# Odd layer: the band mask and the row extreme of the scores move into one VectorE instruction

## What is computed

```
s = q @ k^T * 64**-0.5                 # a block of 128 queries, up to 384 keys
s = where(|i - j| <= 128, s, -inf)     # the band
m = max(max(s, axis=-1), sink)
p = exp(s - m)
p = p / (sum(p) + exp(sink - m))
o = p @ v                              # then a SiLU gate and the output projection
```

## Time and profile before

| | |
|---|---|
| median of three runs | 1152.68 us |
| span of the profiled execution | 1149.1 us |
| rest of the median, around the span | 3.6 us |
| odd layer's scores, first to last | 735.2 to 1122.5 us in the span |
| PE busy | 1123.6 us, 98% |
| DVE busy | 975.0 us, 85% |
| ACT busy | 677.8 us, 59% |
| granted TensorE clock, mean | 0.996 |

### The profile page before, as it was taken

One profiled execution on the slowest core, in us unless ns is written; L12 is line 12 of the kernel. 1 busy time (PEld: TensorE's weight loads), 2 busy tenths in 40 slices (PEclk: granted clock), 3 DMA queues, 4 the chain that ended last, 5 costly groups with the idle time before them and its releaser, 6 DMA issues. The chain is left out here.

```text
span 1149.1 us, 18542 instructions
## 1 busy us (share of the span) xinstructions
PE 1123.6 (98%) x5752; PEld 912.9 (79%) x5752; DVE 975.0 (85%) x1925; ACT 677.8 (59%) x1326; POOL 0.2 (0%) x4
## 2 busy tenths in 40 slices
PE   7999999999999999999999999999999999999996
PEld 6778778778778778778878867887888888888876
DVE  6889889889889889889889898888888888888886
ACT  6475564564554654654654665366666566666664
POOL 0000000000000000000000000000000000000000
PEclk9999999999999999999999999999999999999999
DMA  7614323323224224224125121545232324323111
GB/s 224 165 37 126 113 74 87 97 73 95 88 73 102 80 73 117 65 73 124 59 73 138 47 74 31 122 129 142 61 91 55 91 68 120 98 63 91 55 38 74
DMA packets 131531, 103.62 MB, mean 90 GB/s; under 512 B 5408, under 2 KB 116384, under 8 KB 131488
## 3 DMA queue, kind: packets, MB, share of 16 engines
q1 hardware_dynamic: 131344, 102.81, 32.5%
q10 hardware_dynamic: 144, 0.26, 0.1%
HBM read 77.88 MB, written 2.10 MB: 70 GB/s over the span
## 5 line engine op out<-in xcount | busy, mean ns | idle before, releaser
L74 PE MATMUL bank_proj<-hH,w_hi 128*128 128x512 f32 x856 | 343.0, 401 | 1.2 <-issue 0.8
L76 PE MATMUL bank_proj<-hH,w_lo 128*128 128x512 f32 x856 | 334.8, 391 | 0.0
L75 PE MATMUL bank_proj<-hL,w_hi 128*128 128x512 f32 x856 | 334.5, 391 | 0.0
L76 PEld LDWEIGHTS bank_proj<-hH,w_lo 128*128 128x128 f32 x856 | 161.0, 188 | 35.3
L74 PEld LDWEIGHTS bank_proj<-hH,w_hi 128*128 128x128 f32 x856 | 161.6, 189 | 32.7 <-issue 1.2
L75 PEld LDWEIGHTS bank_proj<-hL,w_hi 128*128 128x128 f32 x856 | 161.6, 189 | 30.6 <-issue 0.2
L2012 ACT ACTIVATE probs<-bank_odd_score,small 128x256 f32<-128x256 f32 (+1 forms) x128 | 66.3, 525 | 73.0 <-DVE small L2263 73.0
L1253 DVE TENSOR_TENSOR w_lo<-w_raw,w_hi 128x1024 fp32r<-128x1024 f32 x74 | 89.6, 1218 | 0.8 <-ACT w_hi L741 0.7
L2019 ACT ACTIVATE probsT<-bank_odd_turn 128x256 fp32r<-128x256 f32 (+1 forms) x128 | 48.8, 434 | 62.8 <-PE bank_odd_turn L1733 62.7
L741 ACT ACTIVATE w_hi<-w_raw 128x1024 fp32r<-128x1024 f32 x74 | 77.9, 1053 | 0.2
L806 ACT ACTIVATE probs<-bank_score,small 128x512 f32<-128x512 f32 x64 | 43.4, 684 | 55.1 <-DVE small L1091 49.3
(11 more groups left out here) (452 smaller groups left out, 2218.8 us busy)
## 6 DMA issues: line engine op xcount, KB each, us to landing
w_raw<-in_w_in_even SPq DMA_DIRECT2D x72, 512.0 KB, 4.7
w_raw<-in_w_in_odd SPq DMA_DIRECT2D x36, 512.0 KB, 4.2
qs<-parts SPq DMA_DIRECT2D x96, 128.0 KB, 2.3
ks<-parts SPq DMA_DIRECT2D x40, 256.0 KB, 4.3
o_raw<-in_w_out_even SPq DMA_DIRECT2D x15, 512.0 KB, 6.1
o_raw<-in_w_out_odd SPq DMA_DIRECT2D x14, 512.0 KB, 6.6
mixT<-in_x SPq DMA_DIRECT2D x2, 512.0 KB, 5.9
attT<-in_x SPq DMA_DIRECT2D x2, 512.0 KB, 6.7
```

The costliest lines, as they stand in the source:

```text
L74: pe.matmul(out, hi, moving_hi, start=start, stop=False)
L75: pe.matmul(out, hi, moving_lo, start=False, stop=False)
L76: return pe.matmul(out, lo, moving_hi, start=False, stop=stop)
```

## The change

The masks leave PE. The band is kept as a float32 tensor of three blocks (left mask, zeros, right mask), of which each tile takes a slice of 2 or 3 blocks. DVE's row maximum becomes one `tensor_tensor_reduce`: it reads the bank and the band, adds them, multiplies by -1/8, writes the result to `probs` in SBUF, and gives the row minimum, which starts from the negated sink. ACT's exponential reads and writes `probs` in place with a scale of -1. The bank `S[a]` is now freed by DVE; a new pair of semaphores (`softened`) tells PE that the exponentials are done. DVE copies the two negated sinks once per half step, into a buffer that the reduction reads as its first value. The wait for the transposes of two tiles before, which frees the buffer `probs`, moves from ACT to DVE. The two casts that made the bfloat16 mask and identity go, and the band's load grows from 2 to 3 blocks.

```diff
@@ scores, PE
-                        mm = pe.matmul(at, query, keys, start=part == 0, stop=False)
-                    if t > 0:
-                        mm = pe.matmul(S[a][:, 0:P], eye_b[:], band[:, 0], start=False, stop=t == NC - 1)
-                    if t < NC - 1:
-                        mm = pe.matmul(S[a][:, (n - 1) * P:n * P], eye_b[:], band[:, 1], start=False, stop=True)
+                        mm = pe.matmul(at, query, keys, start=part == 0, stop=part == 1)
@@ turns, PE
-                    pe.wait_ge(S[a].free.sem, S[a].free.at(h, tile_use(half, t)))
+                    pe.wait_ge(softened[a].sem, softened[a].at(h, tile_use(half, t)))
@@ soft_max, ACT
-                act.wait_ge(neg_peak.sem, neg_peak.at(h, tile_use(half, t)))
                 for a in range(2):
-                    if T[a].full.due(h, tile_use(half, t) - 2):
-                        act.wait_ge(T[a].full.sem, T[a].full.at(h, tile_use(half, t) - 2))
-                    act.activation(probs[:, t % 2, a, 0:n * P], S[a][:, 0:n * P], ACT.Exp, bias=neg_max[:, i:i + 1],
-                                   scale=SCALE, accum_out=row_sum[:, i:i + 1]).then_inc(S[a].free.sem, 1)
+                    at = probs[:, t % 2, a, 0:n * P]
+                    act.wait_ge(S[a].free.sem, S[a].free.at(h, tile_use(half, t)))
+                    act.activation(at, at, ACT.Exp, bias=neg_max[:, i:i + 1], scale=-1.0,
+                                   accum_out=row_sum[:, i:i + 1]).then_inc(softened[a].sem, 1)
@@ DVE
+            def take_sinks(h, half):
+                if S[1].free.due(h, 4 * half - 4):
+                    dve.wait_ge(S[1].free.sem, S[1].free.at(h, 4 * half - 4))
+                dve.tensor_copy(lowest[:, half], neg_sink[:, bass.ds(2 * KT * half + 2 * h, 2)]).then_inc(lowered.sem, 1)
@@ maxima, DVE
+                if t == 0:
+                    take_sinks(h, half)
+                    dve.wait_ge(lowered.sem, lowered.at(h, half + 1))
                 for a in range(2):
                     dve.wait_ge(S[a].full.sem, S[a].full.at(h, tile_use(half, t)))
-                    dve.tensor_reduce(row_max[:, i + a:i + a + 1], S[a][:, 0:n * P], AX_X,
-                                      ALU.max).then_inc(peak.sem, 1)
-                dve.wait_ge(peak.sem, peak.at(h, i + 2))
-                dve.scalar_tensor_tensor(out=neg_max[:, i:i + 2], in0=row_max[:, i:i + 2], scalar=-SCALE, in1=sinks,
-                                         op0=ALU.mult, op1=ALU.min).then_inc(neg_peak.sem, 1)
+                    if T[a].full.due(h, tile_use(half, t) - 2):
+                        dve.wait_ge(T[a].full.sem, T[a].full.at(h, tile_use(half, t) - 2))
+                    dve.sem_inc(mask_go.sem, 1)
+                    dve.tensor_tensor_reduce(out=probs[:, t % 2, a, 0:n * P], in0=S[a][:, 0:n * P],
+                                             in1=band[:, at:at + n * P], scale=-SCALE, scalar=lowest[:, half, a:a + 1],
+                                             op0=ALU.add, op1=ALU.min,
+                                             accum_out=neg_max[:, i + a:i + a + 1]).then_inc(S[a].free.sem, 1)
```

More of the change, by code:

```diff
@@ L1492, in odd_layer @@
         row_squares, row_rstd = sb("row_squares", [P, NC, 2]), sb("row_rstd", [P, NC])
-        band_raw = sb("band_raw", [P, 2, P])
-        band, eye_b = sb("band", [P, 2, P], BF16), sb("eye_b", [P, P], BF16)
+        band = sb("band", [P, 3 * P])
+        lowest = sb("lowest", [P, 2, 2])
         w_final = soft[:, :, :].rearrange("p a t -> p (a t)")
@@ L1500, in odd_layer @@
         swapped = vt[:].rearrange("p (t q) -> p t q", q=P)
-        row_max, neg_max = small[:, 0:16], small[:, 16:32]
+        neg_max = small[:, 16:32]
         row_sum, weight = small[:, 32:48], small[:, 48:64]
@@ L1518, in odd_layer @@
         o_high, o_low = sem("odd_out_weights_high", 2), sem("odd_out_weights_low", 2)
-        peak, neg_peak = sem("odd_row_max", 16), sem("odd_neg_row_max", 8)
+        softened = [sem(f"odd_probs_ready{a}", 8) for a in range(2)]
+        lowered, mask_go = sem("odd_sinks_taken", 2), sem("odd_mask_go")
         roped = sem("odd_roped", 10, 15)
@@ L1644, in _ @@
             sp.dma_start(sink[:], sink_d.broadcast_to([P, 2 * PAIRS])).then_inc(landed.sem, DMA)
-            sp.dma_start(band_raw[:], band_d).then_inc(landed.sem, DMA)
+            sp.dma_start(band[:], band_d).then_inc(landed.sem, DMA)
             move_k(0, -10)
@@ L1788, in first_head @@
                 proj(0, 0, 0, 3)
-                pe.wait_ge(ready.sem, ready.at(0, 3))
                 pe.wait_ge(k_moved.sem, k_moved.at(0, 4))
@@ L2251, in part @@
                                   ALU.subtract).then_inc(roped.sem, 1)
+            def take_sinks(h, half):
+                if S[1].free.due(h, 4 * half - 4):
+                    dve.wait_ge(S[1].free.sem, S[1].free.at(h, 4 * half - 4))
+                dve.tensor_copy(lowest[:, half], neg_sink[:, bass.ds(2 * KT * half + 2 * h, 2)]).then_inc(lowered.sem, 1)
             def maxima(h, half, t):
-                _, n = window(t)
-                i = 8 * half + 2 * t
+                lo, n = window(t)
+                i, at = 8 * half + 2 * t, (lo - t + 1) * P
+                if t == 0:
+                    take_sinks(h, half)
+                    dve.wait_ge(lowered.sem, lowered.at(h, half + 1))
                 for a in range(2):
                     dve.wait_ge(S[a].full.sem, S[a].full.at(h, tile_use(half, t)))
-                    dve.tensor_reduce(row_max[:, i + a:i + a + 1], S[a][:, 0:n * P], AX_X,
-                                      ALU.max).then_inc(peak.sem, 1)
-                dve.wait_ge(peak.sem, peak.at(h, i + 2))
-                sinks = neg_sink[:, bass.ds(2 * KT * half + 2 * h, 2)]
-                dve.scalar_tensor_tensor(out=neg_max[:, i:i + 2], in0=row_max[:, i:i + 2], scalar=-SCALE, in1=sinks,
-                                         op0=ALU.mult, op1=ALU.min).then_inc(neg_peak.sem, 1)
+                    if T[a].full.due(h, tile_use(half, t) - 2):
[5 more added lines that the diff above has]
+                                             accum_out=neg_max[:, i + a:i + a + 1]).then_inc(S[a].free.sem, 1)
             def low_turn(h, half, t):
@@ L2279, in shift_sink @@
             def shift_sink(h, half):
-                dve.wait_ge(neg_peak.sem, neg_peak.at(h, tile_use(half, NC - 1)))
+                for a in range(2):
+                    dve.wait_ge(S[a].free.sem, S[a].free.at(h, tile_use(half, NC - 1)))
                 sinks = sink[:, bass.ds(2 * KT * half + 2 * h, 2)].unsqueeze(1).broadcast_to([P, NC, 2])
@@ L2290, in weigh @@
                 for a in range(2):
-                    dve.wait_ge(S[a].free.sem, S[a].free.at(h, tile_use(half, NC - 1)))
+                    dve.wait_ge(softened[a].sem, softened[a].at(h, tile_use(half, NC - 1)))
                 dve.tensor_tensor(weight[:, at], weight[:, at], row_sum[:, at], ALU.add).then_inc(weighed.sem, 1)
@@ L2350, in _ @@
             dve.tensor_scalar(neg_sink[:], sink[:], -1.0, None, ALU.mult).then_inc(ready.sem, 1)
-            dve.tensor_copy(band[:], band_raw[:]).then_inc(ready.sem, 1)
-            dve.tensor_copy(eye_b[:], eye[:]).then_inc(ready.sem, 1)
-            dve.wait_ge(ready.sem, ready.at(0, 3))
+            dve.wait_ge(ready.sem, ready.at(0, 1))
             rotate(0, -3)
@@ L2456, in shift_pair_sink @@
             def shift_pair_sink(p):
-                dve.wait_ge(neg_peak.sem, neg_peak.at(HEADS - 1, tile_use(1, 2 * p + 1)))
+                for a in range(2):
+                    dve.wait_ge(S[a].free.sem, S[a].free.at(HEADS - 1, tile_use(1, 2 * p + 1)))
                 sinks = sink[:, 2 * KT + 2 * (HEADS - 1):2 * KT + 2 * HEADS].unsqueeze(1).broadcast_to([P, 2, 2])
@@ L2467, in weigh_pair @@
                 for a in range(2):
-                    dve.wait_ge(S[a].free.sem, S[a].free.at(HEADS - 1, tile_use(1, 2 * p + 1)))
+                    dve.wait_ge(softened[a].sem, softened[a].at(HEADS - 1, tile_use(1, 2 * p + 1)))
                 dve.tensor_tensor(weight[:, at], weight[:, at], row_sum[:, at], ALU.add).then_inc(pair_weighed.sem, 1)
@@ L2622, in constants @@
     q, k = i[:, None], i[None, :]
-    band = np.stack([np.where(k >= q, 0.0, MASKED), np.where(k <= q, 0.0, MASKED)], 1).astype(f32)
+    band = np.concatenate([np.where(k >= q, 0.0, MASKED), 0.0 * (q + k), np.where(k <= q, 0.0, MASKED)], 1).astype(f32)
     return {"rope": rope, "levels": levels, "eye": np.eye(P, dtype=f32), "band": band}
```

## The result

The changed kernel takes **1138.9 us** (median of four runs, 1138.25 to 1141.6), the kernel before 1152.0 beside it (1150.56 to 1153.23). The ratio is 0.9895, with an interval of 0.988 to 0.991: 13 us, or 1.05%, faster. Forecast were 1140.2 us, and a span of 1136.6 us; the profiled span is 1136.4.

The account below looks back on a forecast made before the run. PE's streamed columns bound the odd layer, with DVE next. Seven half 0 steps at 0.43 and six half 1 steps at 1.08 gave 9.5, with the ends 12.5 us: from 1152.7 to 1140.2 us, range 1132.5 to 1148.

Parts of the forecast that it names:

- PE's part: Twelve mask products leave PE per half step, saving 1.14 us each half step, 18.2 us over 16.
- the 0.08 behind a mask: In PE's projection: its first matmul behind masks takes 0.31 us, not 0.23; the 0.08 was taken to go with the mask.
- The slack of 0.14 us: At the values of tile 2, PE starts 0.14 us after DVE's low parts end, read as slack.
- the slower rival: DVE's reduction makes two passes, 0.53 us extra distance each; 8.2 us slower, 1160.9 us; chance 0.09.
- x: Extra distance of DVE's new reduction over the 0.465 us of a `tensor_tensor` with 384 columns; taken as 0.15 us.
- The chain in half 0: DVE, ACT, DVE ahead of tile 2's values bind the half 0 step: 24.73 us, giving 0.43 us and not 1.14.
- the other condition: ACT's second exponential starts 0.57 us behind the first, at m + 1.16 + x, if x is under 0.10.
- m: Start of DVE's `maxima` 2 within a half step; in half 0 forecast to go from 17.01 to 16.86 + 2x.
- The wait in half 0: In the longer half step PE waits 0.6 us at the values of tile 2 for DVE's low parts.
- Half 1: Half steps held by PE; DVE's low parts end at 21.84 us, PE wants them at 21.82; each gives 1.08 us.
- The ends: Outside the steady steps, the first step gains 1.7 us and the last half 1.3 us.
- The sensitivity: DVE between `low_turn` 0 and `low_turn` 2: a reduction's extra distance costs 4x per half 0 step.

Follow-up runs that it names:

- experiment 6: Changed kernel with both DVE moves: low part of the second y before the rotated queries' split, second output add behind tile 2's low parts; 1136.75 us, ratio 0.9872.
- experiment 2: Changed kernel with the 192 bfloat16 mask products put back on PE as products of zeros; 1150.14 us, ratio 1.0.
- experiment 1: Kernel before with its mask products left out, DVE and ACT as before; 1146.56 us, ratio 0.9965.
- experiment 4: Changed kernel with DVE making the low part of the second y before the split of the rotated queries in half 0; 1137.94 us in one run.
- experiment 5: Changed kernel with only the add of the second output tile moved behind the low parts of tile 2 on DVE; 1140.69 us in one run.
- experiment 7: Changed kernel with the first step's load of the next weight tile held back until the second key moves have landed; 1140.3 us, ratio 0.991.
- experiment 3: Changed kernel with one DVE copy of two columns behind each reduction, 128 in all; 1141.62 us, ratio 0.9917.

## Why the prediction was right, point by point

**PE's part** was a little more than forecast. Tile 0 has 0.56 us where I worked out 0.57, and the 0.08 behind a mask is gone. In all the masks of a half step cost 1.22 and not 1.14 (experiment 6).

**The slack of 0.14 us** that I read at the values of tile 2 was none. In the changed kernel, where PE waits there, the values also start 0.15 behind the low parts (848.31 to 848.46), so this is what passes between the two and not time to spare. In the kernel before the weight loads were already held at this place, for which DVE's shorter chain gave back 0.05 us per half step (experiment 2). For half 1 the working took 0.04 as that distance, by which DVE was 0.02 late; with 0.14 it would have been 0.12 late. For half 0 it named the 0.14 and then left it out of the sum.

**The reduction** makes one pass, and the slower rival falls. Its distance is 0.465 + 0.07. I had taken x = 0.15 from two small terms. The one for the scalar read from memory, 0.06, fits (609 ns against 549 for a `tensor_tensor`), though no run takes the scalar away. The one for the accumulator read, 0.09, was mis-sized: the instruction is there, as the Trainium skill says ("VectorE: DVE Perf Modes", section "Two Vector instructions with no wait between them"), 82 ns long, but it starts together with the next instruction and delays it by 0.01 at most. My statement that with it x is 0.15 is refuted. The rule of the Trainium skill, "Vector Engine (DVE) Microarchitecture Reference", section "Points that are easy to get wrong", on halved throughput has two sources in SBUF for its case; here one is in a bank, and the pace is full. No run here tells of the case with both in SBUF.

**The chain in half 0** is the step on which the forecast rested. It does end last, but the number is partly luck. Under x = 0.10 it is the other condition that counts: `add_halves` at m + 1.16 + x + 1.50, and m = 16.86 + 2x, so by the formula the step ends at 24.23 + 3x = 24.44. Measured are 24.45. In that sum the 0.14 between the low parts' end and the values is missing: for the kernel before the same terms give 17.01 + 3.31 + 1.52 + 1.02 + 2.17 = 25.03 and not 25.16. With it the formula says 24.58, and for x = 0.15 it would have said 24.87, which is 1.0 us less gain in seven steps. Two more terms make up for it. From m to `add_halves` it is 2.80 where the formula has 2.73. And m is 16.82 into the step where it has 17.00, since DVE's stretch ahead of `maxima` 2 was not without a gap: in the kernel before the low parts of tile 1 start 0.77 behind the low part of `y` (945.01 to 945.78), in the changed one 0.60 (841.46 to 842.06). With the masks alone taken away m is 16.82 too (experiment 1), and with PE's columns put back 17.02 (experiment 2), so this gap was a wait for PE.

**The wait in half 0** I had put in one place, 0.6 us at the values of tile 2. PE stops first for the low part of `y`, 0.28 us at an output tile, and then has only about 0.1 left to wait at the values. I had the DVE row of `y` within the unbroken stretch and didn't ask who waits for it. It changed no number, for the values come last: without the first hold the second is larger (experiment 4). The account of the step closes: 0.28 at the output tile and 0.10 in starting again there, 0.09 at the values and 0.08 in starting again there are 0.55, and the step is 24.46 - 23.91 = 0.55 longer than one in which PE doesn't wait. It would have mattered to anyone who mends only the chain's end (experiment 5).

**Half 1** was forecast at 24.10, with PE and DVE within 0.02 of each other, and is 24.09, but not for that reason. PE alone would be through in 23.91; the low parts of tile 2, which end 21.78 into the step (forecast 21.84), hold it. Too small a saving on PE and too late a chain came out alike.

**The ends** were mis-sized. The steady steps gave 11.1 us in twelve, where the forecast's lengths give 6 x (0.43 + 1.08) = 9.1. The first step was to give 1.7 and gave -0.2. It is bound by the transfer of keys and queries, which I had not priced, and in the profiled execution the keys took 1.0 longer beside an instruction fetch (experiment 7). The 0.84 us that DVE already waited there before was the sign. The last stretch was to give 1.3 and one half 0 step of 0.43, and gave 0.6: PE's waits in it rose from 2.0 us in five places to 3.3, DVE's low parts being late three times. And 1.2 us of the span's 12.7 lie ahead of the odd layer. So the total was closer than its terms: 2.0 too little in the middle, 3.0 too much at the ends, 1.2 by chance. The 3.6 us that I added around the span were mis-sized too: in every run whose span is listed it is 1.7 to 1.9. The median before (1152.7) came from a slower execution than the profiled one, whose span was 1149.1.

**The sensitivity**, 4x per half 0 step, doesn't hold for small x (experiment 3). The prediction had the other condition for x under 0.10 beside it; I didn't use it when I wrote down what experiment 3 should give: a delay behind both reductions acts twice through m, a third time through the first minimum, and the fourth is hidden by ACT's pace until x is 0.10.

## What to carry to other kernels

When work leaves the bounding engine, cut a steady step at each place where that engine could wait for another, and work out the slack at every one, not only at the smallest: here there were two in one step, 6 us apart, and mending either alone left the other. Price the stretch outside the steady steps by its own bound; a transfer that already makes an engine wait there can take the whole gain. Where an instruction waited for the one just before it on the same engine, something independent put between was nearly free (experiment 4). And compare a transfer with the same transfer in other profiles, before you name what it shared with (experiment 7).

## What the runs showed of the hardware

- The add, scale and row minimum with a value from memory is one instruction on DVE: 479 ns for 256 columns and 609 for 384, with one source in a bank and one in SBUF. Its accumulator is read by an instruction of 82 ns that lies beside the next one.
- A copy of two columns adds 0.07 us between two reductions (experiment 3), though it is 160 ns long.
- A stop of PE costs more than the wait. Behind the stop at 842.27 the next matmul starts 0.34 later and not 0.23, and at the values of tile 2 the second one 0.19 behind the first and not 0.12 (experiment 6, without the stop).
- Twelve bfloat16 products of 128 columns among float32 ones cost PE 1.22 us per half step, 0.10 each, though one moves the next start by only 0.04 (905.21 to 905.25 in the kernel before). The rest lies behind them: the second matmul after a mask starts 0.20 or 0.31 behind the first, where it is 0.12 or 0.23 elsewhere.
- On DVE an instruction that waits for the one before it starts later than the 0.60 us that a 128x512 `tensor_tensor` takes of DVE otherwise: 0.82 behind it at 839.56 to 840.38, and 0.73 and 0.88 at two other places of this step (838.83, 835.96). 0.2 is what filling the first gap gave back (experiment 4).
- A transfer of keys took 1.0 us longer in the four profiles in which one 16 KB instruction packet fell 2.6 us behind its issue (experiment 7).
